# Moving twelve adaptation blocks behind the first gather, and adding their bias in the matmul

## The reference

```python
for l in range(2):
    mod = (silu(c) @ w_ada[l] + b_ada[l])          # 6144 values for all tokens
    sh1, sc1, g1, sh2, sc2, g2 = split(mod, 6)
    h = rms_norm(x, norm1_g[l]) * (1 + sc1) + sh1
    ...                                            # projection, pooling, windowed attention
    x = x + g1 * (y @ w_out[l])
    h2 = rms_norm(x, norm2_g[l]) * (1 + sc2) + sh2
    x = x + g2 * peer_ffn(h2, ...)
```

## Time and profile before

| | |
|---|---|
| median of 3 runs | 2418.6 us (2417.43 to 2426.94) |
| the profiled execution | 2418.6 us, its span 2416.8 us |
| PE / DVE / ACT / POOL busy | 2119.9 / 1232.2 / 823.8 / 600.0 us |
| mean granted TensorE clock | 0.951 |
| moved by DMA | 772.25 MB, mean 320 GB/s over the span |

### The profile page before, as it was taken

The page is one execution under the profiler, slowest core; times in us unless marked ns, Lnnn a source line. Parts: engine busy times, 40 slices in busy tenths (PEclk is TensorE's granted clock), DMA queues, the critical chain, the costliest instruction groups (busy, mean ns, idle before and its releaser), DMA issues.

```text
span 2416.8 us, 24315 instructions
## 1 busy us (share of the span) xinstructions
PE 2119.9 (88%) x8264; PEld 1262.6 (52%) x8264; DVE 1232.2 (51%) x2915; ACT 823.8 (34%) x2356; POOL 600.0 (25%) x548
## 2 busy tenths in 40 slices
PE   7888999878989788889887789887999999989998
PEld 4554555434545344555433334435766666866665
DVE  2356777557677666587667576852630001441001
ACT  1234564334454434354444344541320001231000
POOL 1133343323343443233343435440000000000000
PEclk9889999999999988999998989998999999999999
DMA  9989999999999999999999999993343441253320
GB/s 394 408 329 410 410 427 414 427 426 414 426 427 409 410 427 378 381 417 427 412 427 390 418 423 422 427 425 141 139 175 124 172 157 63 85 207 126 153 117 18
DMA packets 108288, 772.25 MB, mean 320 GB/s; under 512 B 12274, under 2 KB 12546, under 8 KB 16003
## 3 DMA queue, kind: packets, MB, share of 16 engines
q0 software_dynamic: 78336, 570.46, 56.7%
q1 hardware_dynamic: 29828, 200.24, 20.9%
HBM read 769.61 MB, written 1.05 MB: 319 GB/s over the span
## 4 chain that ended last, share of the span: by engine, by line
PE 58%; DVE 20%; DMA 15%; ACT 3%; issue 2%; POOL 0%; DVEq 0%; SPq 0%; ACTq 0%; POOLq 0%
PE PS L511 57%; DMA BIG<-in_uv,EID 13%; DVE BIG L1581 7%; DVE BIG L1281 2%; DMA BIG<-in_wq 1%; DVE TI L1530 1%; DVE TI L1525 1%; DVE BIG L1277 1%; DVE BIG L1565 1%; DMA BIG<-in_win 1%; DVE TV L1528 1%; ACT DG L937 1%; PE PS L571 1%; DVE BIG L1526 1%; DVE TI L1546 1%
## 5 line engine op out<-in xcount | busy, mean ns | idle before, releaser
L511 PE MATMUL PS<-BIG,DG 128*128 128x512 f32 x2048 | 997.8, 630 | 195.9 <-ACT DG L937 163.9
L455 POOL DMA_INDIRECT BIG<-in_uv,EID x512 | 582.8, 1138 | 908.4 <-PE PS L511 866.1
L1581 DVE CUSTOM_DVE_ANT_0 BIG<-BIG,H 128x1024 f32<-128x1024 f32 x512 | 627.7, 1226 | 347.6 <-DMA BIG<-in_uv,EID 302.2
L511 PEld LDWEIGHTS PS<-BIG,DG 128*128 128x128 f32 x2048 | 386.4, 199 | 691.6 <-issue 366.5
L511 PE MATMUL PS<-HT,BIG 128*128 128x128 f32 (+1 forms) x2304 | 386.3, 325 | 16.5 <-DMA BIG<-in_wq 12.2
L511 PEld LDWEIGHTS PS<-HT,BIG 128*128 128x128 f32 x2304 | 352.8, 194 | 84.8 <-issue 46.9
L511 PE MATMUL PS<-BIG,HT 128*128 128x256 f32 (+3 forms) x1216 | 306.0, 411 | 20.2 <-DMA BIG<-in_win 9.6
L1126 ACT ACTIVATE AV<-AV 128x1 f32<-128x1 f32 x512 | 102.6, 200 | 554.0 <-DVE AV L1581 553.2
L511 PEld LDWEIGHTS PS<-BIG,HT 128*128 128x128 f32 x1216 | 236.2, 200 | 92.4 <-issue 50.8
L511 PE MATMUL PS<-BIG 128*128 128x512 f32 (+7 forms) x792 | 277.5, 518 | 3.9 <-ACT BIG L1012 2.1
L1281 DVE TENSOR_TENSOR BIG<-BIG 128x256 f32<-128x256 f32 (+1 forms) x96 | 49.3, 514 | 383.5 <-ACT BIG L1262 381.3
(11 more groups left out here) (161 smaller groups left out, 1182.8 us busy)
## 6 DMA issues: line engine op xcount, KB each, us to landing
BIG<-in_win SPq DMA_DIRECT2D x36, 1024.0 KB, 4.9
BIG<-in_wada POOLq DMA_DIRECT2D x32, 1024.0 KB
BIG<-in_wq SPq DMA_DIRECT2D x32, 1024.0 KB
BIG<-in_wup SPq DMA_DIRECT2D x32, 1024.0 KB, 6.9
BIG<-in_wdn SPq DMA_DIRECT2D x32, 1024.0 KB, 4.8
BIG<-in_wout SPq DMA_DIRECT2D x24, 1024.0 KB, 5.6
BIG<-in_wada SPq DMA_DIRECT2D x16, 1024.0 KB
BIG<-in_uv,EID POOLq DMA_INDIRECT x512
```

The lines of the kernel that those rows point to most:

```text
L455: pool.e.indirect_dma_start(out=slot(u), out_offset=None, in_=I[f"uv{l}"], in_offset=bass.IndirectOffsetOnAxis(ap=EID[:, t * 128 + j:t * 1 ...
L511: return pe.e.matmul(dst, a, b, start=start, stop=stop)
L1581: v.e.tensor_tensor_reduce(out=JD, in0=slot(u)[:, 0:1024], in1=H[:, t, :], scale=1.0, scalar=0.0, op0=ALU.mult, op1=ALU.add, accum_out=AV[ ...
```

## The change

Twelve blocks, (0, 20) to (0, 23) and (1, 0) to (1, 7), leave the opening (EARLY 32 -> 20). They become `late` blocks in the beats of tile 0, one every second beat from 2 on, loaded by SP into `in_w` instead of by POOL into `in_g`. The steps of `drive` that held them go, and the second head starts at step 7 of the first instead of 10. For b >= 8 the bias is no longer added by VectorE: `matvec` begins with one more product, a row of 1/32 (OT, 1 x 32) with the bias row (1 x 256), into the first group of partitions. `partial` is now a ScalarE copy for all blocks. The cleared rows are not needed any more, and SP does not wait for them. The late bias rows get four places in BIAS (partitions 0, 32, 64, 96), and a load waits for the product of four blocks before.

```diff
-EARLY = 32
-LATE = [97 + 2 * i for i in range(12)] + [2 * 129 + 10 + 2 * i for i in range(4)]
-BATCH = {(1, 8): (0, 1), (1, 20): (1, 0)}
+EARLY = 20
+LATE = [2 + 2 * i for i in range(12)] + [97 + 2 * i for i in range(12)] + [2 * 129 + 10 + 2 * i for i in range(4)]
+BATCH = {(0, 20): (0, 0), (1, 8): (0, 1), (1, 20): (1, 0)}
...
@@ sp_program, late
-                    if b > 8:
-                        sp.wait_ge(*at("v.part", 1, b - 1))
-                    sp.e.dma_start(BIAS[0:1, :], I["bada"][1:2, b * 256:(b + 1) * 256]).then_inc(*landed("ld_bias", b))
+                    if l == 1 and b >= 8:
+                        if b >= 12:
+                            sp.wait_ge(*at("pe.ada", 1, b - 4))
+                        sp.e.dma_start(BIAS[b % 4 * 32:b % 4 * 32 + 1, :], I["bada"][1:2, b * 256:(b + 1) * 256]).then_inc(
+                            *landed(f"ld_b{b % 4}", b))
...
-            sp.wait_ge(*at("v.zero"))
...
@@ drive
-                if k in range(18, 57, 3) or WHEN["n2"] <= k < WHEN["n2"] + 3:
+                if k in range(18, 57, 3):
                     next(early)
...
-                if k >= 10:
+                if k >= 7:
                     next(h1, None)
-                if k >= 8:
-                    next(early)
...
@@ pe_program, matvec
                 pe.wait_ge(*at("v.crep"))
+                biased = b >= 8
+                if biased:
+                    q = 0 if l == 0 else b % 4 * 32
+                    pe.wait_ge(*(at("ld_mod" if b < 20 else "ld_g2", 0) if l == 0 else at(f"ld_b{b % 4}", b)))
+                    row = adapt_out(0, b)[0:1, :] if l == 0 else BIAS[q:q + 1, :]
+                    mm(PS[0:32, bk, 0:256], OT[q:q + 1, :], row, True, False)
                 pe.wait_ge(*at(("ga%d" if ring is in_g else "ld%d") % u, *key))
...
@@ pe_program, pre and experts
-                if l == 1:
+                if (l, t) == (0, 1):
+                    pe.wait_ge(*at("v.col", 1, 7))
+                elif l == 1:
...
-                    pe.wait_ge(*at("a.ada", 0, 23))
-                    pe.wait_ge(*at("v.col", 1, 7))
+                    pe.wait_ge(*at("a.ada", *ADA[EARLY - 1]))
...
@@ act_program, partial: the copy for every b
-                if b < 8:
-                    a.wait_ge(*at("pe.ada", l, b))
-                    if n > 1:
-                        a.wait_ge(*at("pe.adb", *ADA[n - 2]))
-                    copy(ACC[:, b % 2, 0:256], PS[:, banks.where[("ada", l, b)], 0:256]).then_inc(*up("a.part", l, b))
+                a.wait_ge(*at("pe.ada", l, b))
+                if n > 1:
+                    a.wait_ge(*at("pe.adb", *ADA[n - 2]))
+                copy(ACC[:, b % 2, 0:256], PS[:, banks.where[("ada", l, b)], 0:256]).then_inc(*up("a.part", l, b))
...
@@ dve_program: partial goes, late takes the columns of b < 8, no cleared rows
-                    tt(ACC[:, b % 2, 0:256], PS[:, banks.where[("ada", l, b)], 0:256], adapt_out(0, b) if l == 0 else BIAS, ALU.add).then_inc(
-                        *up("v.part", l, b))
...
-                    yield from k.to(LATE[i] + 2)
-                    partial(*x, in_b)
+                    yield from k.to(LATE[i] + 4)
+                    modulation(*x, in_b)
...
-            v.e.memset(MOD[:, 2048:5120], 0.0)
-            v.e.memset(BIAS, 0.0)
-            v.e.memset(G2, 0.0).then_inc(*up("v.zero"))
...
+            v.e.memset(OT, 1.0 / 32)
```

More of the change, by code:

```diff
@@ L186, in build @@
         CREP = MOD[:, 128:384].rearrange("p (k m) -> p k m", k=8)
-        MC, BC, NC = MOD[:, 0:32], MOD[:, 32:64], MOD[:, 64:80]
+        MC, BC, NC, OT = MOD[:, 0:32], MOD[:, 32:64], MOD[:, 64:80], MOD[:, 96:128]
         SC = sb("SC", 384)[:, :]
@@ L442, in pool_program @@
             for l, b in ADA[0:EARLY]:
-                if (l, b) == (0, 8):
+                if b == 8:
                     pool.wait_ge(*at("pe.proj", 0, 0, PROJ[0]))
@@ L524, in matvec @@
                     j = k % 4 * 32
-                    p = mm(PS[j:j + 32, bk, 0:256], CREP[:, k, :], w[:, k, :], k < 4, k >= 4)
+                    p = mm(PS[j:j + 32, bk, 0:256], CREP[:, k, :], w[:, k, :], k < 4 and not (biased and k == 0), k >= 4)
                 p.then_inc(*up("pe.ada", l, b))
@@ L530, in spread @@
                 bk, R = banks.where[("ada", l, b)], ACC[:, b % 2, 0:256]
-                pe.wait_ge(*at("a.part" if b < 8 else "v.part", l, b))
+                pe.wait_ge(*at("a.part", l, b))
                 if b < 8:
@@ L539, in early @@
             def early():
-                for blocks in (ADA[0:8], ADA[8:20], ADA[20:EARLY]):
+                for blocks in (ADA[0:8], ADA[8:EARLY]):
                     for i, x in enumerate(blocks):
@@ L1320, in early @@
             def early():
-                for blocks in (ADA[0:8], ADA[8:20], ADA[20:EARLY]):
-                    for i, x in enumerate(blocks):
-                        partial(*x, in_a)
+                for blocks in (ADA[0:8], ADA[8:EARLY]):
+                    for i in range(len(blocks)):
                         if i > 0:
```

## The result

The changed kernel is slower: a median of 2447.6 us (6 runs, 2441.8 to 2453.2), against 2421.3 us (6 runs, 2417.4 to 2426.9) of the kernel before, measured beside it; the ratio is 1.0108, with a 95% interval of 1.0089 to 1.0128. The profiled execution took 2444.4 us around a span of 2442.7 us, 25.9 us more than the span before.

What follows compares the result with a forecast made beforehand. It took the first block as fed by DMA and the second by TensorE. +29.5 - 0.1 - 4.8 - 0.5 = +24.1 us on the profiled 2418.6 us gave 2442.7 us; 8-in-10 range 2429 to 2454.

Steps and rivals of the forecast that it cites:

- Bytes are time among the gathers: Tile 0: twelve blocks, 12.58 MB, loaded under a full DMA at 427 GB/s, cost +29.5 us.
- The ramp: Right behind the first gather's issue: with all eight slots free, the present slow DMA start goes, -0.5 us.
- The first gather stays: End of the opening: the first gather stays at about 143.4 us, -0.1 us (bounds -7.3 to +5.4).
- Bias product: Opening, TensorE: one more K=1 product per block at 0.4 us, some 9 of 12 on the path, +3.6 us.
- TensorE's clock in the head: First head: TensorE idles some 5 us, then runs transposes and query product at half clock, +3.0 us (0 to +4.3).
- Score copy: First head: ScalarE's copy after the key product no longer queues behind a block's modulation, -1.8 us.
- VectorE in the head: First MAX8 to the gather's issue: VectorE's waits for a block's column sums go, -4.0 us (-3.1 to -4.5).
- Bias loads: Tile 2: SP's freer bias loads remove a late `win` block and the idle DMA, -4.8 us (0 to -4.8).
- Products among the gathers: Behind the opening: 28 bias products and copies lie under a full DMA and cost nothing; 11 us if TensorE were the limit.
- That the gathers aren't bound by DMA: Rival: a loop of slot, dot product and matmul binds the gathers; earlier first product, 2406 us, not slower; chance 0.05.
- Late weights: Rival: weights through SP's four slots in tile 0 land late and stall TensorE; three give +38 us, 2457; chance 0.08.
- Slower by less: Rival: tile 0 has room up to 427 GB/s and absorbs 7 us; about +10 us, 2428; chance 0.12.

Runs made afterwards that it cites:

- experiment 2: Changed kernel, but the twelve moved blocks load only 256 of their 2048 columns, all products kept: 2432.7 us, ratio 1.0065 to the kernel before.
- experiment 5: Changed kernel, with POOL's queue loading eight more 1 MB blocks that nobody reads before the first gather: 2448.4 us, ratio 1.0121 to the kernel before.
- experiment 7: Changed kernel with eight blocks moved instead of twelve, (0,20) to (0,23) staying in the opening: 2435.3 us, ratio 1.0074 to the kernel before.
- Experiment 6: Changed kernel without the bias products of the twelve blocks that stay in the opening: 2440.8 us, ratio 1.0092 to the kernel before.
- experiment 4: Changed kernel, with SP's bias load waiting for the copy of the block before it again: 2457.7 us, ratio 1.0161 to the kernel before.
- experiment 3: Changed kernel, but the twelve moved blocks do four of their eight products, all loads kept: 2448.8 us, ratio 1.0124 to the kernel before.
- experiment 1: Changed kernel with its twelve blocks put back into the opening, leaving the bias as a matmul and freer bias loads: 2423.0 us, ratio 1.0018.
- experiment 9: Experiment 8 with VectorE adding the bias in the opening again, bias products for the 16 late blocks only: 2419.4 us, ratio 1.0006.
- experiment 8: Experiment 1 (all 32 blocks early) with ten of the opening's last steps moved behind the first head's indices: 2414.0 us, ratio 0.9980.
- experiment 10: The kernel of experiment 8 unchanged, run again on another chip: 2418.0 us, ratio 1.0007 to the kernel before.

## Why the prediction was right

It said 2442.7 us (2429 to 2454), slower with 0.83; 2447.6 us was measured, and the profiled execution's 2444.4 us stand against a sum of 2442.7. Step by step:

*Bytes are time among the gathers* (+29.5): tile 0 grew by 30.3 us. Experiments 2, 5 and 7 show it from three sides. The twelve blocks were not literally all in tile 0, as three are still loaded before the first gather; but they push a `wq` and two `win` blocks of SP's ring behind it in exchange, and the sum of bytes, which is what counts, was 12.61 MB for the predicted 12.58. The blocks also changed from POOL's queue to SP's; no run separates that, but tile 0's mean rate did not fall (417 and 421 GB/s).

*The ramp* (-0.5): wrong. It should have gone, since all eight slots are free. But the first 5 us behind the first gather's issue look as they did, before and after:

```profile
143.37:148.37 5.00, 4.70 (x36) 2.12 (x36) 0.16 (x1) 0.66 (x2) 3.84 (x4) 0.50 0.65 224
```

```profile
141.32:146.32 5.00, 0.00 (x0) 0.00 (x0) 1.54 (x9) 0.00 (x0) 3.83 (x4) 0.50 0.65 226
```

*The first gather stays* (-0.1, bounds -7.3 to +5.4): -2.05 us. The parts were:

- Bias product (+3.6): the transposes before the output projection began at 98.63 us, 4.1 us later than before. From its start to the start of the next product it takes 0.55 us (50.92 to 51.47 us), above the upper bound of 0.50 and not the 0.4 that I took. My mistake was to leave room for an overlap between column groups, though I had written that the next product, on the same group, has to follow. The Trainium skill (TensorE: Matmul & The Clock Gate, Why this matters for your kernels) says that one matmul of small K takes as long as one with K=128, and that the gain comes from running several side by side. The trace agrees roughly: 0.55 us is near the 0.44 us of two of the projection's full records (14.08 us for 64), and far from the 0.13 us that I had as the lower bound.
- Transposes and output projections (not foreseen): they took less time, since TensorE's clock was already up this time. From the start of the first norm's transposes to that of the projection are 2.49 us (98.63 to 101.12); before they were 3.47: -1.0. The projection takes 14.08 us for 15.90: -1.8. The windows show a clock of 1.00 at 98 to 100 us, where it was 0.50. Experiment 6 has both back: no bias products, and a projection of 15.71 us at the lower clock.
- Second norm (-0.9): from the projection's end to the transposes -0.8.
- TensorE's clock in the head (+3.0): the transposes took 1.97 us for 1.09 and the query product 6.40 for 3.81: +0.9 and +2.6.
- Score copy (-1.8): from the end of the key product at 130.90 us ScalarE needs no time to begin its copy, and the first MAX8 begins 0.46 us behind that end, 1.9 us sooner than before.
- VectorE in the head (-4.0): from the first MAX8 (131.36 us) to the gather are 9.96 us instead of 14.08: -4.1.

They add up to +4.1 -1.0 -1.8 -0.8 +0.9 +2.6 -1.9 -4.1 = -2.0 us. The sum of the term was good to 2 us partly by luck, as two misses (a product too cheap, a clock not foreseen) had opposite signs.

*Bias loads* (-4.8, bounds 0 to -4.8): right in mechanism (experiment 4), a little small in size. The hole was worth 5.0 us. Tile 2 as a whole became 6.5 us shorter for the same bytes (157.18 and 157.21 MB), and in experiment 4 9.0 us longer. The other 1.5 us is not placed. The bound left no room beyond the one hole.

*Products among the gathers* (0): experiment 3 shows it for half of the moved blocks' products; the bias products there were not tested by themselves.

The rivals. That the gathers aren't bound by DMA would have needed a tile 0 that stays at 413 us (the prediction wrongly says about 380); it takes 443.5. The first product did come 8.3 us earlier (149.07 us, and 157.38), as this rival foresaw with 7.6, and nothing was gained by it. The gather landed 5.3 us after its issue, not 4: the changed kernel's first dot product begins at 146.64 us, when its wait for the gather ends. Late weights: TensorE has no wait for a weight left between the first gather and the end of tile 2. Slower by less: the mean rate in tile 0 rose from 417 to 421 GB/s, so 1% of 443 us, 4 us, was room, not the 7 us of the rival. But tile 0 also moved 14.5 MB more (172.17 and 186.63 MB), 1.9 MB of them loads that used to fall into tile 1, and tile 1, with 1.8 MB less to move, was 0.8 us longer: in 20 us at the turn of the tiles (590 to 610 us, 561 to 581 us before) DMA moved 318 GB/s instead of 390. Both tiles together grew by 31.1 us for 12.7 MB, 407 GB/s, so that no room is left in the sum.

The other signs came as foretold: 40.99 MB before the first gather, a DMA share of 0.44 over 90 to 95 us, a query product at the lower clock, and a second block that begins 24.5 us later.

What stays open is small. The last +3.3 us (tile 3 and the second block) can't be told from the spread of the runs: tile 3 takes 334.6 to 338.5 us and the second block 769.8 to 771.4 us over all kernels, before it 335.7 and 769.8. Why DMA was short for 2.9 us more in experiment 1's tile 0 than before, and for 7.7 us more in experiment 9's, isn't placed. And whether the version of experiments 8 and 10 is 0.2% faster isn't settled.

## What to carry to other kernels

A full DMA share doesn't say that a stretch is bound by DMA: ask whether what ends the stretch waits for the bytes. The opening had a share of 1.01 over 20 to 100 us and still was a chain of TensorE and VectorE work, from which 12.6 MB could be taken without making it more than 2 us shorter (and 8.4 MB of unread loads could be put back at no cost); the gathers had the same share, and there every megabyte cost 2.4 us. So loads belong into stretches that something else binds, and the test is cheap: load something that nobody reads and see whether the time moves. The waits of an engine that issues DMAs deserve the same look: one bias row's wait on SP made a weight late and left DMA idle for 5 us.

## What the runs showed of the hardware that I had not expected

- A K=1 product of 256 columns in 32 of 128 columns of the array takes 0.61 us by its record and 0.55 us from start to start, half of what the sixteen records of a whole block take (1.07 us), as these run four abreast.
- The opening's length varies with TensorE's clock though TensorE's work in it is the same. In experiments 8 and 10, the same kernel, the first gather was issued at 139.01 and 144.49 us, with a granted clock of 1.00 and 0.71 over 100 to 110 us. In five kernels that differ in the opening by loads alone (experiments 2 to 5 and the changed one) it was issued between 140.5 and 146.3 us. In experiment 3, the latest, the granted clock was 0.71 over 100 to 110 us, and a bias product took 1.05 us:

```profile
98.41 1.05 PE L511 MATMUL PS<-MOD 1*32 1x256 f32 x2 [0.47 <-ACT MOD L945]
99.40 1.93 PE L511 MATMUL PS<-BIG,MOD 128*32 128x256 f32 x16
...
106.67 14.08 PE L511 MATMUL PS<-BIG,HT 128*128 128x256 f32 x64 [0.96 <-ACT HT L945]
```

  One profile's start can be off by 5 us, while tile 0 took 443.5 to 445.8 us in those of the five that load all their bytes.
- The first block runs at 427 GB/s for whole slices. The Trainium skill (DMA: Bandwidth & Descriptors, Bandwidth) gives 425 GB/s for 16 MB and 341 for a lone 1 MB; transfers of 1 MB with several in flight came out at the former here.
